# Query and key features of the heads in another order, rotated ones swapped by ScalarE in place of a product with signs; tokens in four transfers; another order of work at the start

## What is computed

```python
xn = rms_norm(x, norm_w)
aq, ak, av, az, mq, mk, mv, mo, mz, ga, gm, mi, mf = split(xn @ w_in)       # 11 x 1024 columns and 8
aq = partial_rope(rms_norm(aq per head of 128, q_norm_w), pos)              # ak alike with k_norm_w
# partial_rope: of each head's 128 features the first 32 are rotated:
#   x1, x2 = x[0:16], x[16:32];  out = [x1*cos - x2*sin, x2*cos + x1*sin, x[32:]]
attn  = causal attention of the prompt (8 heads); of each sample over 3 of 4 blocks of its paged cache, chosen by a gate
h, C, n, m = mLSTM (4 heads of 256), prompt in chunks and one step per sample on stored states
y = x + (sigmoid(ga) * (attn*silu(az)) @ w_proj_attn + sigmoid(gm) * (norm(h)*silu(mz)) @ w_proj_mlstm) @ w_out
```

## Time and profile before

| what | value |
|---|---|
| median, lowest, highest of 3 runs | 481.1, 480.91, 483.06 us |
| the profiled execution's own time | 482.34 us |
| its span, first to last instruction | 480.2 us |
| TensorE (PE) busy | 462.4 us, 96% |
| VectorE (DVE) busy | 403.8 us, 84% |
| ScalarE (ACT) busy | 290.0 us, 60% |
| GpSimd (POOL) busy | 101.3 us, 21% |
| moved by DMA | 150.86 MB, mean 314 GB/s |

### The profile page before, as it was taken

The page is one execution under the profiler, slowest core; times in us unless marked ns, Lnnn a source line. Parts: engine busy times, 40 slices in busy tenths (PEclk is TensorE's granted clock), DMA queues, the critical chain, the costliest instruction groups (busy, mean ns, idle before and its releaser), DMA issues.

```text
span 480.2 us, 11312 instructions
## 1 busy us (share of the span) xinstructions
PE 462.4 (96%) x3848; PEld 420.8 (88%) x3848; DVE 403.8 (84%) x1650; ACT 290.0 (60%) x486; POOL 101.3 (21%) x181
## 2 busy tenths in 40 slices
PE   3899999999989999989999999999999999999997
PEld 2699899898879899889899989989889898999997
DVE  2878899789999898999999999979999973577861
ACT  2776555586884485785665595558757458234430
POOL 2031312112323221532322242222223110000000
PEclk9999999999999999999999999999999999999999
DMA  8399489748799999999999999998999996546521
GB/s 315 149 351 365 145 324 332 259 158 311 230 415 418 408 364 332 328 380 415 415 404 329 377 404 394 412 393 308 339 420 407 417 413 250 176 155 238 186 85 46
DMA packets 36377, 150.86 MB, mean 314 GB/s; under 512 B 5200, under 2 KB 6740, under 8 KB 29024
## 3 DMA queue, kind: packets, MB, share of 16 engines
q1 hardware_dynamic: 12160, 70.77, 38.8%
q0 software_dynamic: 19008, 67.20, 36.5%
q10 hardware_dynamic: 5152, 12.18, 6.5%
HBM read 137.37 MB, written 12.76 MB: 313 GB/s over the span
## 4 chain that ended last, share of the span: by engine, by line
PE 72%; DVE 19%; DMA 3%; issue 3%; ACT 2%; ACTq 0%; DVEq 0%
PE pj L515 28%; PE pj L518 14%; PE wk L515 8%; DVE w L1037 5%; DVE kpages L1144 4%; PE pa L708 4%; PE wk L518 4%; DVE cslot L1230 4%; DMA out_C_s<-cslot 2%; PE wk L482 2%; PE wk L620 2%; PE wk L652 1%; PE pa L494 1%; PE wk L523 1%; PE wk L524 1%
## 5 line engine op out<-in xcount | busy, mean ns | idle before, releaser
L515 PE MATMUL pj<-xn,w 128*128 128x264 f32 x1344 | 183.2, 289 | 2.9 <-ACT mqT L946 2.9
L515 PEld LDWEIGHTS pj<-xn,w 128*128 128x128 f32 x1344 | 170.6, 189 | 11.5 <-issue 6.8
L1037 DVE TENSOR_TENSOR w<-wraw,w 128x1024 fp32r<-128x1024 f32 x112 | 136.9, 1225 | 10.9 <-ACT w L792 10.4
L792 ACT ACTIVATE w<-wraw 128x1024 fp32r<-128x1024 f32 x112 | 117.8, 1053 | 27.6 <-PE wk L518 12.8
L1144 DVE CUSTOM_DVE_ANT_0 kpages<-kpages,qbc 128x128 f32<-128x128 f32 x512 | 114.6, 286 | 3.4 <-DMA kpages<-in_cache_k 3.3
L518 PE MATMUL pj<-xn,w 128*128 128x264 f32 x672 | 95.4, 284 | 1.6 <-DVE w L1037 1.6
L518 PEld LDWEIGHTS pj<-xn,w 128*128 128x128 f32 x672 | 86.5, 188 | 2.3 <-DVE w L1037 2.2
L399 POOL DMA_DIRECT2D kpages<-in_cache_k x64 | 34.3, 536 | 180.6 <-DVE sco L1144 152.5
L399 POOL DMA_DIRECT2D vpages<-in_cache_v x64 | 33.9, 530 | 67.4 <-issue 39.0
L1144 DVE DVE_READ_ACCUMULATOR2_ANT sco<- 128x1 f32 x512 | 40.5, 79 | 0.0
L708 PE MATMUL pa<-vpages,prob 128*32 128x256 f32 x512 | 34.3, 385 | 0.8 <-ACT prob L851 0.8
(11 more groups left out here) (269 smaller groups left out, 637.8 us busy)
## 6 DMA issues: line engine op xcount, KB each, us to landing
wraw<-in_weights SPq DMA_DIRECT2D x56, 1024.0 KB, 8.0
kpages<-in_cache_k POOLq DMA_DIRECT2D x64, 512.0 KB, 8.5
vpages<-in_cache_v POOLq DMA_DIRECT2D x64, 512.0 KB, 10.6
cslot<-in_states SPq DMA_DIRECT2D x16, 512.0 KB, 11.0
out_C_s<-cslot ACTq DMA_DIRECT2D x16, 512.0 KB, 8.5
xres<-in_tokens SPq DMA_DIRECT2D x1, 1056.0 KB, 7.5
out_k_p<-kT ACTq DMA_DIRECT2D x4, 256.0 KB, 11.8
out_v_p<-v_nat ACTq DMA_DIRECT2D x4, 256.0 KB, 6.3
```

Source lines behind the costliest of these rows:

```text
L515: mm(bank[:, 0:T], w2[:, q, 0, k, :], src[:, g, k, :], start=(k == 0 and g == 0), stop=False)
L792: A(w2[:, n % WSPLIT, 0], wraw[:, pair % WRAW, :, (n % 2) * P:(n % 2 + 1) * P], ACT.Copy).then_inc(whi_ready, 1)
L1037: V.tensor_tensor(w2[:, q, 1], wraw[:, slot, :, half * P:(half + 1) * P], w2[:, q, 0], ALU.subtract).then_inc(wlo_ready, 1)
```

## The change

- The features of each query and key head are stored in the order `ORDER`: the first 16 rotated ones on partitions 0 to 15, the other 16 on partitions 32 to 47, so that the pairs are 32 partitions apart. Columns of the weights, the norms' weights, cos and sin (which now carries the signs) are laid out so beforehand, and the keys are put back in order on the host. The samples' query rows are brought back to the old order by a product with a permutation `back` in place of the transpose.
- `norm_sums` has no product with `rot`. Instead `head_copy` has ScalarE copy partitions 32 to 63 of the head to 0 to 31 of a new tile `swapped`, and 0 to 31 to 32 to 63 (two instructions of 32x264). The first three passes of `rope_norm` go over 64 partitions and not 128, the fourth over all.
- The mLSTM's inverse root has a tile of its own, `mrs`; ScalarE's wait for `mlg_ready` moves from the key heads' `inv_rms` to `output_gate`, where it is a job older.
- The tokens come in four transfers, two by SyncE and two by ScalarE; VectorE squares and adds quarter by quarter. TensorE does six fp32 products of zeros (`qmask`) before the first sum. All of the tokens are scaled before their low parts are formed, and the first low part of weights goes ahead of those; two small memsets move behind them. ScalarE rounds the first weights before the tokens. The first projection is done in the order w_hi*x_hi, w_lo*x_hi, w_hi*x_lo.

```diff
@@ sync
-            sp.dma_start(xT[:, 0:4, :].rearrange("p k t -> p (k t)"), a["tokens"][:, 0:4 * T]).then_inc(boot_x[0], 16)
+            for part in (0, 2):
+                sp.dma_start(xT[:, 2 * part:2 * part + 2, :].rearrange("p k t -> p (k t)"),
+                             a["tokens"][:, 2 * part * T:2 * (part + 1) * T]).then_inc(boot_x[part], 16)
@@ tensor
+            pe.wait_ge(blank, 3)
+            for _ in range(BLANKS):
+                mm(wk[3][:, 0:NB * VC], qmask[:, 0, 0:P], qmask[:, 0, :], start=True, stop=True)
+
             pe.wait_ge(boot_c, 16)
...
+                if parts:
+
+                    for k in range(KC):
+                        pe.wait_ge(xhi_ready, k // 2 + 1)
+                        mm(bank[:, 0:T], w2[:, q, 0, k, :], src[:, 0, k, :], start=(k == 0), stop=False)
+                    pe.wait_ge(wlo_ready, n + 1)
+                    for k in range(KC):
+                        mm(bank[:, 0:T], w2[:, q, 1, k, :], src[:, 0, k, :], start=False, stop=False)
+                    for k in range(KC):
+                        pe.wait_ge(parts, k + 1)
+                        last = mm(bank[:, 0:T], w2[:, q, 0, k, :], src[:, 1, k, :], start=False, stop=(k == KC - 1))
+                    last.then_inc(proj, 1)
+                    return
...
-            def norm_sums(ss, ro, i, src):
-
-                mm(ss[:, 0:T], ones, sq[:, i, :], start=True, stop=True)
-                mm(ro[:, 0:T], rot, src, start=True, stop=True).then_inc(norm_ps, 1)
+            def norm_sums(ss, i):
+                mm(ss[:, 0:T], ones, sq[:, i, :], start=True, stop=True).then_inc(norm_ps, 1)
...
                     if g >= 2:
-                        pe.wait_ge(q_ready, g - 1)
-                    norm_sums(wk[2 * (g % 2)], wk[2 * (g % 2) + 1], g % 2, qT[:, g, :])
+                        pe.wait_ge(rs_ready, g - 1)
+                    norm_sums(wk[2 * (g % 2)], g % 2)
...
-                    last = tr(bank[0:NB, (h - first) * P:(h - first + 1) * P], qT[:, h, SEQ:T], P)
+
+                    last = mm(bank[0:NB, (h - first) * P:(h - first + 1) * P], qT[:, h, SEQ:T], back, start=True, stop=True)
@@ scalar
+            split_hi(0)
             for p in range(KC // 2):
-                if p == 1:
-                    split_hi(0)
...
-            def head_copy(n, dst, w, i):
+            def head_copy(n, dst, w, i, turn):
 
                 act.wait_ge(proj, n + 1)
-                A(dst, pj[n % 2][:, 0:T], ACT.Copy, scale=w)
+                ch.step(A(dst, pj[n % 2][:, 0:T], ACT.Copy, scale=w))
                 A(sq[:, i, :], pj[n % 2][:, 0:T], ACT.Square).then_inc(evac, 1)
+
+                ch.join()
+                act.wait_ge(swap_read, max(0, turn - 1))
+                A(swapped[0:LO, i, :], dst[LO:2 * LO], ACT.Copy)
+                A(swapped[LO:2 * LO, i, :], dst[0:LO], ACT.Copy).then_inc(swap_ready, 1)
...
                 act.wait_ge(mln_ps, j + 1)
-                act.wait_ge(kT_ready, 2 * j + 2)
-                inv_rms(wk[3][:, 0:T], rs[:, 0, :], MHD).then_inc(mrs_ready, 1)
+                act.wait_ge(mlg_ready, j)
+                inv_rms(wk[3][:, 0:T], mrs[:, :], MHD).then_inc(mrs_ready, 1)
...
                     n2 = i // 2 - 1
-                    act.wait_ge(mlg_ready, j)
+                    act.wait_ge(kT_ready, 2 * j)
@@ vector
-                if k in (3, 5):
-                    dve.wait_ge(xn_ready, k - 1)
-                    x_lo(k // 2 - 1)
+            split_lo(0)
             dve.wait_ge(xn_ready, KC)
-            x_lo(2)
-            x_lo(3)
-            split_lo(0)
+            for p in range(KC // 2):
+                x_lo(p)
...
-            def rope_norm(x, r, ro, done):
-
-                ch.step(V.tensor_tensor(hT[:, 0, :], ro[:, 0:T], sin, ALU.mult))
-                ch.link(V.tensor_tensor(x, x, cos, ALU.mult))
-                ch.link(V.tensor_tensor(x, x, hT[:, 0, :], ALU.add))
+            def rope_norm(x, r, i, done, turn):
+                part = slice(0, 2 * LO)
+                dve.wait_ge(swap_ready, turn + 1)
+                V.tensor_tensor(hT[part, 0, :], swapped[:, i, :], sin[part], ALU.mult).then_inc(swap_read, 1)
+                ch.link(V.tensor_tensor(x[part], x[part], cos[part], ALU.mult))
+                dve.wait_ge(swap_read, turn + 1)
+                ch.link(V.tensor_tensor(x[part], x[part], hT[part, 0, :], ALU.add))
                 V.tensor_tensor(x, x, r, ALU.mult).then_inc(done, 1)
```

More of the change, by code:

```diff
@@ L222, in build @@
         rsum = sb("rsum", [P, 2, 2])
+        mrs = sb("mrs", [P, T])
+        swapped = sb("swapped", [2 * LO, 2, T])
         pj = [ctx.enter_context(nc.psum_tensor(f"pj{i}", [P, 512], F32)) for i in range(2)]
@@ L271, in build @@
         boot, boot_c, boot_r, boot_n, boot_g = sem("boot"), sem("boot_c"), sem("boot_r"), sem("boot_n"), sem("boot_g")
-        boot_x = [sem(f"boot_x{i}") for i in range(2)]
+        boot_x = [sem(f"boot_x{i}") for i in range(4)]
         blank, blank_eye = sem("blank"), sem("blank_eye")
@@ L774, in _ @@
             act.sem_inc(mrs_ready, 1)
-            act.dma_start(xT[:, 4:8, :].rearrange("p k t -> p (k t)"), a["tokens"][:, 4 * T:8 * T]).then_inc(boot_x[1], 16)
+            for part in (1, 3):
+                act.dma_start(xT[:, 2 * part:2 * part + 2, :].rearrange("p k t -> p (k t)"),
+                              a["tokens"][:, 2 * part * T:2 * (part + 1) * T]).then_inc(boot_x[part], 16)
             nc.scalar.preload_act_table_set("natural_log_exp_and_others")
             for half in range(2):
-                act.wait_ge(boot_x[half], 16)
+                act.wait_ge(boot_x[2 * half], 16)
                 part = slice(4 * half, 4 * half + 2)
@@ L1040, in _ @@
             for half in range(2):
-                dve.wait_ge(boot_x[half], 16)
+                dve.wait_ge(boot_x[2 * half + 1], 16)
                 part = slice(4 * half + 2, 4 * half + 4)
-                ch.step(V.tensor_tensor(xsq[:, part], xT[:, part], xT[:, part], ALU.mult))
-            ch.join()
-            for half in range(2):
+                ch.link(V.tensor_tensor(xsq[:, part], xT[:, part], xT[:, part], ALU.mult))
                 dve.wait_ge(xsq_act, half + 1)
-                part = slice(4 * half + 2, 4 * half + 4)
                 V.tensor_tensor(xsq[:, part], xsq[:, part], xsq[:, 4 * half:4 * half + 2], ALU.add).then_inc(xsq_dve, 1)
-            dve.wait_ge(blank, 6)
-            ch.step(V.memset(gpad[:, NBLK:, :], 3.0e38))
-            ch.step(V.memset(pairs[:, :, 0:NBLK - 1, :], 0.0))
             dve.wait_ge(boot, 16)
@@ L1422, in constants @@
     half = ROT // 2
-    for m in range(half):
-        c[m + half, C_ROT + m] = -1.0
-        c[m, C_ROT + m + half] = 1.0
+    c[np.arange(P), C_BACK + ORDER] = 1.0
     r = np.arange(P)
@@ L1454, in weight_pairs @@
 def weight_pairs(w_in, w_proj_mlstm, w_proj_attn, w_out):
-    cuts = [w_in[:, AQ + 256 * n:AQ + 256 * (n + 1)] for n in range(4)]
-    cuts += [w_in[:, g + 256 * j:g + 256 * (j + 1)] for j in range(JOBS) for g in GROUPS]
+    pair = np.concatenate([ORDER, HD + ORDER])
+    cuts = [w_in[:, AQ + 256 * n + pair] for n in range(4)]
+    cuts += [w_in[:, g + 256 * j + (pair if g == AK else np.arange(256))] for j in range(JOBS) for g in GROUPS]
     for w in (w_in[:, GA:GA + D], w_in[:, GM:GM + D], w_proj_mlstm, w_proj_attn, w_out):
@@ L1500 @@
     y = g["y"].reshape(P, KC, T).transpose(2, 1, 0).reshape(T, D)
-    k_p = g["k_p"].transpose(3, 0, 2, 1).reshape(rows)
+    there = np.argsort(ORDER)
+    k_p = g["k_p"][:, there].transpose(3, 0, 2, 1).reshape(rows)
     v_p = g["v_p"].reshape(JOBS, P, 2, 256).transpose(2, 1, 0, 3).reshape(rows)
```

42 lines of the change are left out of this document (21 added, 21 removed).

## The result

The changed kernel takes 483.57 us in the median of 20 runs (482.08 to 487.08), the kernel before 481.73 in 20 runs beside them (480.74 to 484.58). The ratio is 1.0042 with a 95% interval of 1.0023 to 1.0061: slower by 0.4%, about 1.8 us, where 0.9% faster was forecast. The time is outside the range.

The account below looks back on a forecast made before the run. The body was taken to be bound by VectorE and TensorE in turn. The terms 2.8 + 1.5 + 0.9 + 0.1 + 0 - 1.1 = 4.2 us took 481.1 to 476.9 us, range 473.2 to 480.4.

Parts of the forecast that it names:

- start, up to S: Kernel start: earlier additions and products of zeros bring S from 12.63 to 9.8; gain 2.8, ends 0.5 and 3.2.
- S: Start of VectorE's first L1067, the first use of the tokens' norm: 12.63 before, 9.8 forecast.
- S to the query rows: Query heads: VectorE becomes the bound, TensorE resumes at S + 39.1 in place of S + 40.6; gain 1.5.
- the query rows themselves: After the query heads: the queries' transposes become products of the same shape; nothing gained or lost.
- job 0, two products with signs: Job 0, where TensorE works without a wait: two removed products, 2 x 0.45 = 0.9 gained.
- job 2: Beginning of job 2: ScalarE's removed wait of 1.37 against 1.42 us added; nothing gained.
- job 3: Beginning of job 3: ScalarE 1.42 - 0.18 = 1.2 later, removed products count for nothing; 1.1 lost.
- (a): Kernel start: with four transfers VectorE's additions end at about 7.2 in place of 8.07; +0.9.
- ScalarE becomes the bound: ScalarE's chains at the heads and jobs' beginnings bound, slower than before; 483.8 at 0.64 per copy; chance 0.08.
- c: Price in us of one crossing copy on ScalarE: 0.33 taken; "ScalarE becomes the bound" decides from 0.55.
- The transfers' rival: Kernel start: four transfers land later than two, constants and weights too; gain 3.1, 478.0; chance 0.10.
- The other rivals: Clock low during the start's sums: 479.2, chance 0.15; TensorE bounds everywhere: 469.4, or half-way 473.5, chance 0.14.

Follow-up runs that it names:

- free copies: Changed kernel with no crossing copy at all, the tile of swapped features set to zero once: 477.03 us.
- the start alone: Kernel before with only the start's changes (four token transfers, zero products, new order of additions, splits and first projection), heads unchanged: 477.04 us, ratio 0.9899.
- straight copies: Changed kernel with the same two copies of 32 partitions, but each to its own partitions, without crossing: 482.5 us in one execution.
- the inserted wait: Kernel with the start alone, plus six idle VectorE passes before the last query head's rotation, nothing beside them on TensorE: 481.59 us.

## Why the prediction was wrong

In the order of its sum, with the profiled execution's measured terms:

| step | forecast | measured |
|---|---|---|
| start, up to S | 2.8 | 2.84 |
| S to the query rows | 1.5 | 0.7 |
| the query rows themselves | 0 | -0.9 |
| job 0, two products with signs | 0.9 | 0.9 |
| job 1 | 0.1 | 0 |
| job 2 | 0 | -0.7 by ScalarE, -1.2 by the clock |
| job 3 | -1.1 | -1.9 by ScalarE, -2.7 by the clock |
| sum | 4.2 | -3.0 |

Of the 7.2 us between the two sums, 3.9 are the clock in the jobs, 1.5 ScalarE's lateness there beyond the forecast, 0.9 the query rows, 0.8 the stretch up to them and 0.1 job 1.

- *Held: the start.* S at 9.79, sums without the slow pace, the first projection's end 7.3 behind S, (a) worth 0.9. That eight products with signs would be hidden by VectorE held too: with free copies TensorE comes to the last query head 7.0 us ahead and resumes 5.6 ahead (47.63 for 53.22), having waited 2.3 us for VectorE. That is S + 37.4, against S + 38.8 with the start alone: 1.4 of the 3.6 us that eight products take. Without the heads' part all of the start's gain is kept.
- *Mis-sized: the crossing copy, 0.33 us.* It is the first step that failed. I took it from the earlier trace rows, an instruction on 128 partitions whose successor starts 0.09 before its end, and set the two copies that close. They measure 0.43 and 0.45 to their successors and the first starts 0.39 behind the square, 0.12 later than what follows the square otherwise: 0.50 apiece. I had the rival that goes by this number, with +1.5 for the whole sum at 0.5, but gave it 0.08 and took the earlier trace rows for its far end. The Trainium skill, page "ScalarE: Activation LUTs", section "What ACT_TABLE_LOAD costs", has instructions in a row overlap by about 93 ns; the distance of L814 to L856 agrees with it (0.33 for 0.42 us of work), these copies don't (0.43 and 0.45 for 0.42).
- *Mis-sized with it: S to the query rows.* VectorE's first rotation starts at S + 14.6, where S + 14.3 was forecast: with the start alone it is S + 12.6, and the two pairs of copies ahead of the first inverse root take the 2.0 back. From there to the query rows it is 25.3 us where 24.8 was forecast, with VectorE waiting 0.5 for ScalarE before its seventh rotation. The forecast wait of TensorE came, but 2.7 of its 3.1 us are for ScalarE's last square and only 0.4 for VectorE.
- *Mis-sized with it: jobs 2 and 3.* At 1.00 a pair, ScalarE is 2.0 later in place of 1.4, less the removed wait: 2.0 - 1.37 = 0.6 in job 2 and 2.0 - 0.18 = 1.8 in job 3, against 0.7 and 1.9 measured. The mechanism, the chain and the place are those of the prediction.
- *Missed: the query rows, 0.9 us on the path.* "Products of the same shape: nothing" looked at shapes and not at records: the earlier trace rows shows four transposes as x4, while the earlier trace rows counts a product as x2.
- *Missed altogether: the clock, the largest term.* The prediction foresaw the wait of 3 us at the query heads (2.72 + 0.36 came) and a wait over 1 us in job 3 and costed both at their own length. What follows such a wait was nowhere in the sum, since nothing in the profile of before waits in mid-kernel for more than 1.5 us, and the clock was looked at only at the start. At the query heads the fall costs 0.3 at most, since VectorE is next there anyway (lead 2.64 after it, and without a fall there 2.94 in the run with straight copies and 2.67 in the one without the key heads' copies). In the jobs it costs 3.9. Without falls the changed kernel would, by this estimate, take 484.7 less 1.5 (tail) less 3.9 less 0.3: a span of 479.0, 481.1 with what lies around it, about the time of the kernel before. So the mis-sized copies and the missed rows eat the start's gain, and the clock makes it a loss.
- The rival "ScalarE becomes the bound" named the right engine and the side; for c = 0.50 it says +1.5, but its own terms give 2.8 - 0.1 + 0.9 - 2.4 = +1.2; less the 0.9 of the rows that is +0.3, where the leads without falls give +1.2. The difference is the resumption, S + 40.7 by its formula and S + 39.9 measured. It had no term for the clock, so it put the point of decision at 0.55. The transfers' rival has a slip of 0.2 too: 4.2 less 1.3 is 2.9 and not 3.1; nothing hangs on it. The other rivals fell: the clock rose before the sums, TensorE isn't the bound, four transfers were not later.

Open: why a fall comes in one execution and not in the other at a wait of 2.7 us, and why it lasts 6.8 us in job 3 of the changed kernel and 3.4 everywhere else; and 0.6 to 0.9 us of lead that the version with the start alone gains on the kernel before in jobs 2 and 3.

## What to carry to other kernels

Price an instruction that is added to an engine's queue by the distance between its start and its successor's, with and without it; a neighbour of another shape or with another operand gave 0.33 here for what cost 0.50. A wait of TensorE of about two us or more in mid-kernel was here followed by work at half pace in 11 of 19 cases, at a price of up to 2.7 us; it is to be costed with that, and where it can't be removed, some products beside it can pay for themselves (481.34 against 483.57). And a change of several parts is measured in parts: one of these was worth 4.8 us, the other cost 6.5, and together they gave a small loss.

## What the runs showed of the hardware

- ScalarE copies of 32x264 took 0.42 us and started 0.42 to 0.45 before their successors, without overlap, crossing partitions or not; crossing cost 0.13 more, once per pair and ahead of the first copy.
- TensorE's granted clock fell at some waits in mid-kernel and not at others. In the profiled executions it fell at eight of twelve waits of 2.3 to 3.4 us, at three of seven of about 2.0, and at none of the shorter ones (five of 1.7 to 1.8 among them). Each fall but one lasted 3.4 us, one 6.8. With the inserted wait of 3.4 us all ten executions have a mean clock below 1.00; where it falls is shown for the profiled one alone.
- Five executions of the kernel before in the three sets, none of them profiled, have 0.996. They took 484.44 to 486.43 us, some 3 to 4.6 above their medians, more than one fall of 3.4 us cost in any profiled execution; what waited there isn't known.
- With the zero products the executions of the start-only version lie within 0.4 us (four of them), without them within 4.6 (ten): with products that compute nothing the time was steadier as well. That the moment at which the clock rises sets this spread is likely and wasn't shown.
